# Moving the arena by 96 bytes and the input's low part to rooms at other distances in a two-block transformer kernel

## The reference, cut to what matters

```python
def swiglu(x, w_in, w_out):
    gate, up = jnp.split(x @ w_in, 2, axis=-1)
    return (jax.nn.silu(gate) * up) @ w_out

for layer in range(DEPTH):                      # DEPTH = 4, D_MODEL = 1024, D_FF = 2816
    g = norm_g[layer]
    ff = swiglu(rmsnorm(h, g[0]), ffn_w_in[layer, 0], ffn_w_out[layer, 0])
    h = h + 0.5 * rmsnorm(ff, g[1])
    ...                                         # the mixer
    ff = swiglu(rmsnorm(h, g[4]), ffn_w_in[layer, 1], ffn_w_out[layer, 1])
    h = h + 0.5 * rmsnorm(ff, g[5])
```

## Time and profile before

| | |
|---|---|
| median of 3 timed runs | 3413.98 us (3413.7 to 3414.19) |
| the profiled execution's own time | 3409.92 us |
| its span, first to last instruction | 3408.1 us |
| mean granted TensorE clock | 0.99 |
| instructions profiled | 49,870 |
| TensorE matmuls, busy | 21,454, 3286.4 us (96%) |
| VectorE busy | 1962.3 us (58%) |
| ScalarE busy | 1516.1 us (44%) |
| GpSimd busy | 175.0 us (5%) |
| HBM read | 516.21 MB, mean 153 GB/s |

### The profile page before, as it was taken

The page is one execution under the profiler, slowest core; times in us unless marked ns, Lnnn a source line. Parts: engine busy times, 40 slices in busy tenths (PEclk is TensorE's granted clock), DMA queues, the critical chain, the costliest instruction groups (busy, mean ns, idle before and its releaser), DMA issues.

```text
span 3408.1 us, 49870 instructions
## 1 busy us (share of the span) xinstructions
PE 3286.4 (96%) x21454; PEld 2902.6 (85%) x21454; DVE 1962.3 (58%) x2964; ACT 1516.1 (44%) x2539; POOL 175.0 (5%) x201
## 2 busy tenths in 40 slices
PE   7999999999999999999999999999999999999998
PEld 7987998987898987686989988987878888887897
DVE  5556545558555555674555565555456555825777
ACT  4455445455444443113444464454544344524554
POOL 0000000003000000230000000000011000100100
PEclk9999999999999999999999999999999999999999
DMA  7563656554656544314556554551013333531452
GB/s 252 185 197 105 217 189 213 186 178 156 216 186 217 186 150 156 124 44 154 186 189 220 181 163 160 187 175 28 26 62 112 122 125 124 176 96 62 136 186 99
DMA packets 413481, 522.06 MB, mean 153 GB/s; under 512 B 41639, under 2 KB 355740, under 8 KB 413132
## 3 DMA queue, kind: packets, MB, share of 16 engines
q1 hardware_dynamic: 407376, 515.92, 46.0%
q0 software_dynamic: 816, 2.10, 0.2%
q10 hardware_dynamic: 5068, 0.85, 0.1%
HBM read 516.21 MB, written 2.10 MB: 152 GB/s over the span
## 4 chain that ended last, share of the span: by engine, by line
PE 87%; DVE 7%; ACT 4%; issue 1%; POOL 0%; ACTq 0%; DMA 0%; DVEq 0%; POOLq 0%
PE ps L187 24%; PE ps L188 24%; PE ps L189 24%; PE ps L179 5%; PE ps L1332 2%; PE ps L197 2%; ACT junk L723 1%; DVE tmp L706 1%; PE ps L2044 1%; DVE fast_xt L776 1%; ACT a L1352 1%; DVE small L1389 1%; PE ps L3916 1%; PE ps L3913 1%; PE ps L869 0%
## 5 line engine op out<-in xcount | busy, mean ns | idle before, releaser
L187 PE MATMUL ps<-a 128*128 128x256 f32 (+1 forms) x4832 | 1521.0, 315 | 23.4 <-DVE fast_xt L776 8.6
L189 PE MATMUL ps<-a 128*128 128x256 f32 (+1 forms) x4664 | 1459.9, 313 | 0.0
L187 PEld LDWEIGHTS ps<-a 128*128 128x128 f32 x4832 | 923.4, 191 | 87.0 <-DVE a L1062 10.9
L188 PE MATMUL ps<-fast_xt,a 128*128 128x256 f32 x3400 | 964.2, 284 | 0.0
L189 PEld LDWEIGHTS ps<-a 128*128 128x128 f32 x4664 | 890.7, 191 | 52.7
L992 DVE TENSOR_TENSOR a<-ring,a 128x1024 fp32r<-128x1024 f32 x594 | 693.7, 1222 | 345.9 <-ACT a L986 345.9
L986 ACT ACTIVATE a<-ring 128x1024 fp32r<-128x1024 f32 x594 | 585.9, 1049 | 233.7 <-PE ps L189 233.6
L188 PEld LDWEIGHTS ps<-fast_xt,a 128*128 128x128 f32 x3400 | 652.9, 192 | 7.5
L188 PE MATMUL ps<-a 128*128 128x512 f32 (+1 forms) x1368 | 529.0, 387 | 0.0
L188 PEld LDWEIGHTS ps<-a 128*128 128x128 f32 x1368 | 258.7, 189 | 43.7
L1094 ACT ACTIVATE tmp<-ps 128x256 f32<-128x256 f32 x176 | 67.6, 384 | 496.8 <-PE ps L189 496.8
(11 more groups left out here) (380 smaller groups left out, 3925.2 us busy)
## 6 DMA issues: line engine op xcount, KB each, us to landing
ring<-in_ffn_w_in_dram SPq DMA_DIRECT2D x218, 1024.0 KB, 7.4
ring<-in_ffn_w_out_dram SPq DMA_DIRECT2D x121, 1024.0 KB, 5.0
ring<-in_ada_w_dram SPq DMA_DIRECT2D x48, 1024.0 KB, 5.3
ring<-in_swa_w_qkv_dram SPq DMA_DIRECT2D x12, 1024.0 KB, 8.0
ring<-in_gla_w_in_dram SPq DMA_DIRECT2D x12, 1024.0 KB, 7.1
ring<-in_rwkv_w_rkv_dram SPq DMA_DIRECT2D x12, 1024.0 KB, 5.1
ring<-in_na_w_qkv_dram SPq DMA_DIRECT2D x12, 1024.0 KB, 6.3
ring<-in_swa_w_o_dram SPq DMA_DIRECT2D x8, 1024.0 KB, 5.7
```

The costliest lines, as they stand in the source:

```text
L187: pe.x.matmul(out, lh, rh, start=start and i == 0, stop=False)
L188: pe.x.matmul(out, lh, rl, start=False, stop=False)
L189: ins = pe.x.matmul(out, ll, rh, start=False, stop=stop and i == n - 1)
```

## The change

`small` has 24 columns less, so that what stands behind it, the arena included, stands 96 bytes lower. And `ffn_memory` looks up a pair (high, low) for the branch, in columns of 4 bytes: so many columns are left free ahead of xh and ahead of a room of its own for the low part, xl. In the eight branches of the table the low part is thus no longer in `fast_xt`. The two numbers and the rest behind xl make 128 columns, so that ht and hs stand 512 bytes further from the pieces than before in these branches. Branches 0 and 8 are not in the table; in branch 0 the low part stays in `fast_xt`. The code of the engines is the same.

```diff
+PLACE = {1: (0, 8), 2: (0, 16), 3: (0, 32), 4: (0, 40), 5: (0, 48), 6: (0, 56), 7: (32, 0), 10: (24, 40)}
+
+
 def ffn_memory(K, f, w_in, w_out):
     c = Core()
     c.w_in, c.w_out = w_in, w_out
     c.pieces = [(K.arena(1024, F32R), K.arena(1024, F32R)) for _ in range(6)]
-    c.xs = v3(K.arena(2048, F32R), T), v3(K.fast_xt[:, 0:2048], T)
-    K.arena(2048)
+    high, low = PLACE.get(f, (0, None))
+    if high:
+        K.arena(high)
+    xh = K.arena(2048, F32R)
+    if low is None:
+        xl = K.fast_xt[:, 0:2048]
+        K.arena(2048 - high)
+    else:
+        if low:
+            K.arena(low)
+        xl = K.arena(2048, F32R)
+        K.arena(128 - high - low)
+    c.xs = v3(xh, T), v3(xl, T)
     c.ht = [K.arena(T) for _ in range(2)]
     c.hs = [(K.arena(T, F32R), K.arena(T, F32R)) for _ in range(LATE)]
...
-        K.smallbuf = sb("small", 640)
+        K.smallbuf = sb("small", 616)
```

## The result

The changed kernel takes 3395.43 us (median of 5 runs, 3392.94 to 3397.77) against 3413.86 for the kernel before (5 runs, 3409.39 to 3414.19). The ratio is 0.9949, its 95% interval 0.9934 to 0.9963: faster by about 17 to 18 us, where the forecast was no change. The profiled execution took 3394.17 us, 15.75 less than that of before, at the same mean granted clock of 0.99.

What follows compares the result with a forecast made beforehand. The prediction took the spacing of TensorE matmul starts as the bound; its terms, 0 + 0 + 0, left the profiled 3409.92 us unchanged, and the forecast was put on the timed median, 3414.0 us, range 3395 to 3431.

Steps and rivals of the forecast that it cites:

- What bounds the kernel: Inside a branch only the spacing of TensorE matmul starts sets the time: 8.50 us a turn, 0.120 per 256-column matmul.
- the 13 ns that are not columns: Of each 120 ns 256-column spacing, 107 are columns; the remaining 13 are what changed addresses can win or make larger.
- Parts 1 and 2: Arena 96 bytes lower with its inner distances kept, and low input part in its own 8 KB: 0 us taken for each.
- Part 3: Changed distances between moving operand and next weights for 4,448 split-product matmuls: value 0, bounds 31 us gained and 36 us lost.
- The 16-column weights: Rows with 16-column weights start off multiples of 256 bytes yet keep 116 ns, taken as evidence that distance is worth nothing.
- the rival's gain: If distance helped, line 188 alone would be short in branches 1 to 6, all three lines in 7; 15 us, chance 0.31.
- Faster by distance: TensorE's two reads meet in the same memory part, always at distance 0; scattered distances gain 15 us: 3399, chance 0.31.
- Slower by scatter: Equal distances lock the even pace; affected matmuls off 256-byte multiples pay 3.3 ns, 15 us: 3429, or 3450; chance 0.14.
- Slower by alignment: Operand starts count: all arena operands 32 bytes off 64-byte multiples cost 3.3 ns on 14,184 matmuls, 47 us: 3461; chance 0.06.
- The rule on ports: TensorE's two independent SBUF read ports never wait, so distance is worth nothing and the time stays.
- The criterion: Prediction wrong if any branch's turn leaves 8.50 us by more than 0.03, since 22 turns in nine branches make 6 us.

Runs made afterwards that it cites:

- the first kernel: Separate kernel without the computation: TensorE alone issues streams of 96 matmuls (48 where wide) at various operand shifts; all at 0 gave 120.0 ns a matmul.
- the rooms alone: Changed kernel with `small` back at 640 columns, so the arena stands where it was and only the input parts' rooms differ: 3399.61 us, ratio 0.9954.

## Why the prediction was wrong

**What bounds the kernel.** Right. Only the spacing of matmul starts sets the time of a branch; the nine branches took 17.4 us less, and the rest 1.6 more. So was the bill of the 13 ns that are not columns: they are what the addresses moved.

**Parts 1 and 2 as operations.** Right, at 0. A shift of the arena that keeps distances changes no turn, and a room of its own for the low part changes neither line 776 nor the turn.

**Part 3, the value 0.** This is the step that failed. The term that it put at nothing measured 16.1 us of gain by the turns: 3.8 ns on each of the 4,224 affected matmuls of the nine branches. The other 224, in mixers, went from 120.0 to 117.3 ns. The bounds around it, 31 gained and 36 lost, held. The count left something out: the 512-column matmuls of the mixers between the arena and the ring or `fast_xt` moved as well, and lost 3 us. Each of the reasons for 0 was an inference from rows that could not carry it:

- "The spacing is the same to a nanosecond whatever lies beside what." It is, but every one of those distances was a multiple of 64 columns. The text said so itself two paragraphs earlier. Rows that all sit at one value of a variable say nothing on that variable.
- The 16-column weights. Weights of 64 or 32 columns take 113.4 and 113.3 ns at distance 0 and are slowed, to 116.3 and 116.7, by the shift that shortens 128-column ones from 120.0 to 117.9. Narrow weights were no stand-in for wide ones; they answer the other way.
- "Most of the 13 ns are there with hardly any load to collide with", so a limit of feeding the array. From 120.0 to 113.3 ns is half of the surplus over 106.7, and it goes away either with weights of at most 64 columns or with 28 columns of distance. So half of it is no fixed limit of feeding the array. That the load is what it hangs on is an inference from these two, not shown by itself.

**Where it would show.** The text put the rival's gain on line 188 alone. All three lines got shorter: in the steady turns of branch 0, where only the low part moved, lines 187, 188 and 189 have 117.8, 117.5 and 117.9 ns. In branch 1 the shifted line 188 has 118.5 and its neighbours 116.4 and 116.3. A shifted matmul changes the time at which its neighbours begin. And branch 7, where the rival had all three lines short, is the one that got slower.

**Faster by distance.** The nearest of the rivals, at a chance of 0.31: the distance does set the pace, and its 15 us stand against 16.1 by the turns and 15.75 between the profiled executions. The size is in good part luck. Half of 7 ns was a guess for a spread of distances, and the gain came on other lines than it said, and in other shares. Its reason, that both reads meet in the same part of the memory and do so all the time at distance 0, is not shown by any run, and "120 is the slowest" did not hold: 1 column has 123.2 ns, (24, 24) has a turn of 8.527.

**Slower by scatter.** Half right. At 512 columns nothing beats distance 0, and all others tried but 60 columns cost 229 to 235 ns; in the mixers this cost 3 us. For 256 columns, which are 80% of the matmuls of a turn, distance 0 lies in the middle: of the 64 distances 28 have under 119.5 ns, 18 over 120.5 and 18 about its 120. The reason that the text gave for the uneven 512-column rows, VectorE and ScalarE emptying PSUM, is not needed: TensorE alone shows 231 to 233 ns in all six streams of the first kernel in which a distance is not 0. The first spacings after the 256-column ones are uneven with it alone too: a turn at (16, 16) has 2.757 us for its 12, as the branch has.

**Slower by alignment.** Out, by the rooms alone, and by the streams in which a shift of both operands changes nothing.

**The rule on ports.** The Trainium skill, "SBUF — State Buffer", Who interferes with whom, says that TensorE reads moving operand and weights through two independent ports and never waits. By it all turns would have stayed at 8.50 us. The same instructions with other addresses gave 8.21 to 8.53, so the measurement decides against it here. The Trainium skill, "TensorE: Matmul & The Clock Gate", Back-to-back issue gap, gives the 109 ns for 256 columns as the gap of a matmul by itself, and says that in a stream of weight loads and matmuls both set the spacing. No stream here reached 109; the shortest steady spacing of 256 columns is 113.3.

**The criterion.** The text called itself wrong if any branch's turn left 8.50 by over 0.03 us. Eight of nine did.

## What to carry to other kernels

Where TensorE is the bound and fp32r matmuls with 256 moving columns and 128-column weights follow each other, the distance between the two operands inside a partition was worth up to 5.6% of their time here (113.3 ns against 120.0). Other types were not tried. It costs nothing to try: in this kernel 28 columns (112 bytes) for both parts gave a ratio of 0.9835 with not one instruction changed. Measure the loop's whole turn, since most distances that help 256 columns cost at 512, and the same move reaches every stage whose tiles it shifts, and the pace depends on what ran before; and before an old row is taken as proof that a parameter is worth nothing, look whether the parameter ever had another value in it.

## What the runs showed of the hardware

- Steady spacings at full clock with 128-column weights at distance 0 are 146.6, 173.3 and 226.7 ns for 320, 384 and 512 moving columns, and 120.0 for 256. At 2.4 GHz the columns alone would be 133.3, 160.0, 213.3 and 106.7, so the surplus is 13.3 ns whatever the length. With weights of at most 64 columns, or at 28, 36 or 48 columns of distance, it is 6.7 at 256 columns.
- For 512 moving columns the distances from 4 to 56 columns cost 229 to 235 ns, and 60 columns 227.0.
- For 256 columns at other distances the spacings repeat in a short pattern (five at 32 columns, four at 8), and their mean lies between 113.3 and 123.2.
- The pace has a memory. The same shift of 8 columns gave 117.9 ns in the first of three turns and 116.7 in the next two. At 48 columns a long stream of TensorE alone settles at 113.3, the same 48 after a down product stay at 117.8, and with the hidden tiles moved as well the pace is 113.9 in eight branches and 117.8 in one.
- What stays open is the law. No run derives the pace from the distances: the next weights are not the only partner, and pairs of shifts do not add. Whether a shift of the weights alone would do as well in the kernel was not tried. Why branch 7 fell to the second pace, and whether ScalarE and VectorE hold 48 columns at 117.8, stays open.
